# A landing wait in the expert gather: GpSimd issues a pair of rows only when the rows five and six places back have landed

## The reference, cut to what matters

```python
v1, i1 = lax.top_k(s[:, :, 0], PEER_TOPK)      # 16 best of 128 keys, twice
v2, i2 = lax.top_k(s[:, :, 1], PEER_TOPK)
...
sc, p = lax.top_k(cand, PEER_TOPK)             # 16 best of the 256 pairs
eidx = jnp.take_along_axis(cidx, p, axis=-1)
gates = jax.nn.softmax(sc, axis=-1)
ue = u[eidx]
ve = v[eidx]
act = jax.nn.gelu(jnp.einsum('td,thkd->thk', xb, ue).astype(jnp.float32), approximate=False)
return jnp.einsum('thk,thkd->td', (gates * act).astype(x.dtype), ve)
```

## Time and profile before

| | |
|---|---|
| median of 3 runs | 1628.4 us (1625.92 to 1628.66) |
| the profiled execution | 1629.01 us |
| its span, first to last instruction | 1627.2 us |
| mean granted TensorE clock over the span | 0.957 |
| busy: PE, DVE, POOL, ACT | 86%, 63%, 36%, 31% |
| first row of the gather issued, last one issued | 198.59 us, 964.87 us |

### The profile page before, as it was taken

The page is one execution under the profiler, slowest core; times in us unless marked ns, Lnnn a source line. Parts: engine busy times, 40 slices in busy tenths (PEclk is TensorE's granted clock), DMA queues, the critical chain, the costliest instruction groups (busy, mean ns, idle before and its releaser), DMA issues.

```text
span 1627.2 us, 20312 instructions
## 1 busy us (share of the span) xinstructions
PE 1400.7 (86%) x7520; PEld 1041.9 (64%) x7520; DVE 1022.3 (63%) x1818; ACT 497.4 (31%) x846; POOL 586.4 (36%) x630
## 2 busy tenths in 40 slices
PE   8899967977776777587778779999999998999998
PEld 7788956622222222242224329999999997899998
DVE  5995758756546456484744346777877547555444
ACT  2232101211111211121111117554443667544432
POOL 1320055466666666676666550012221002100000
PEclk9999978799998999899999899999999999999999
DMA  9956597799999999999999995758996443245450
GB/s 377 328 209 242 193 370 274 298 366 366 363 370 339 368 365 392 347 368 367 338 371 367 361 352 204 266 207 325 321 317 230 143 150 110 78 156 182 172 188 26
DMA packets 114077, 454.15 MB, mean 279 GB/s; under 512 B 12048, under 2 KB 29600, under 8 KB 100816
## 3 DMA queue, kind: packets, MB, share of 16 engines
q0 software_dynamic: 81616, 297.84, 48.5%
q1 hardware_dynamic: 32384, 155.31, 26.2%
HBM read 452.06 MB, written 1.05 MB: 278 GB/s over the span
## 4 chain that ended last, share of the span: by engine, by line
PE 55%; POOL 12%; issue 11%; DMA 9%; DVE 9%; another core or an unknown queue 3%; ACT 2%; SPq 0%; DVEq 0%; POOLq 0%; ACTq 0%
PE psum L2194 15%; POOL arena L514 12%; PE psum L1818 8%; PE psum L2208 8%; DMA arena<-v_d,arena 7%; PE psum L2089 6%; PE psum L1774 4%; PE psum L1761 3%; DVE arena L1355 3%; PE psum L1849 1%; PE psum L1833 1%; PE psum L1876 1%; PE psum L2049 1%; PE psum L1758 1%
## 5 line engine op out<-in xcount | busy, mean ns | idle before, releaser
L2089 PE MATMUL psum<-arena 128*128 128x512 f32 x952 | 484.4, 643 | 157.4 <-DMA arena<-v_d,arena 109.8
L2089 PEld LDWEIGHTS psum<-arena 128*128 128x128 f32 x952 | 174.7, 199 | 463.8 <-DMA arena<-v_d,arena 261.8
L1355 DVE CUSTOM_DVE_ANT_0 arena<-arena,psum 128x1024 f32<-128x1024 f32 x256 | 304.4, 1219 | 191.1 <-DMA arena<-u_d,arena 158.2
L514 POOL DMA_INDIRECT arena<-u_d,arena x256 | 242.4, 947 | 242.5 <-issue 71.1
L514 POOL DMA_INDIRECT arena<-v_d,arena x256 | 241.1, 942 | 81.9 <-issue 72.9
L741 ACT ACTIVATE arena<-ident,arena 128x128 f32<-128x128 f32 x238 | 84.9, 394 | 445.2 <-PE psum L2089 234.0
L1030 DVE TENSOR_TENSOR wlo<-ring,whi 128x2048 fp32r<-128x2048 f32 x69 | 158.1, 2292 | 86.4 <-ACT whi L582 86.4
L2194 PE MATMUL psum<-xh,whi 128*128 128x256 f32 x704 | 202.1, 287 | 1.3 <-DVE xl L1024 1.0
L2194 PE MATMUL psum<-xl,whi 128*128 128x256 f32 x704 | 199.2, 283 | 0.0
L2194 PE MATMUL psum<-xh,wlo 128*128 128x256 f32 x704 | 199.1, 283 | 0.0
L582 ACT ACTIVATE whi<-ring 128x2048 fp32r<-128x2048 f32 x69 | 131.2, 1902 | 23.7 <-PE psum L1818 18.9
(11 more groups left out here) (309 smaller groups left out, 2317.1 us busy)
## 6 DMA issues: line engine op xcount, KB each, us to landing
ring<-w_ffn SPq DMA_DIRECT2D x44, 1536.0 KB, 6.9
second<-w_ada POOLq DMA_DIRECT2D x64, 384.0 KB, 6.1
arena<-w_ada SPq DMA_DIRECT2D x50, 384.0 KB, 8.5
ring<-w_inproj SPq DMA_DIRECT2D x14, 1024.0 KB, 7.4
ring<-w_qkv SPq DMA_DIRECT2D x12, 1024.0 KB, 4.8
ring<-w_l0in SPq DMA_DIRECT2D x10, 1024.0 KB, 6.8
ring<-w_peerq SPq DMA_DIRECT2D x8, 1024.0 KB, 6.4
sq<-w_ada SPq DMA_DIRECT2D x14, 384.0 KB, 7.4
```

The lines of the kernel that those rows point to most:

```text
L514: g.indirect_dma_start(S["rows"][:, p % GRING, :], None, u_d if kind == "u" else v_d, bass.IndirectOffsetOnAxis(S["idx"][:, n // SLOTS, n ...
L1355: v.tensor_tensor_reduce(row, row, xrow[n // SLOTS], 1.0, 0.0, ALU.mult, ALU.add, S["act"][:, n // SLOTS, n % SLOTS:n % SLOTS + 1]).then_i ...
L2089: ins = t.matmul(vacc[tt][:, at], S["diag"][:, c % DIAGS, :], row[:, at], start=(n % SLOTS == 0), stop=(n == LAST_PE[tt]))
```

## The change

POOL gets one more condition ahead of each pair from p = 6 on: the rows at p - 6 and p - 5 must have landed. It is told by the counts of their semaphores. The circle keeps its 16 buffers, and all other waits stay.

```diff
@@ -61,6 +61,7 @@
 GRING = 16
 DIAGS = 8
+FLIGHT = 6
@@ -511,6 +512,9 @@
                         pool.wait_ge(v_used, pe_count(b))
                     if dve_count(b) > dve_count(a):
                         pool.wait_ge(v_dve, dve_count(b))
+                if p >= FLIGHT and p % 2 == 0:
+                    for q in (p - FLIGHT, p - FLIGHT + 1):
+                        pool.wait_ge(row_in[q % GRING], 16 * (q // GRING + 1))
                 g.indirect_dma_start(S["rows"][:, p % GRING, :], None, u_d if kind == "u" else v_d,
                                      bass.IndirectOffsetOnAxis(S["idx"][:, n // SLOTS, n % SLOTS:n % SLOTS + 1], 0)
                                      ).then_inc(row_in[p % GRING], 16)
```

## The result

The changed kernel took 1619.7 us (median of 12 runs, 1607.6 to 1627.0) and the kernel before 1627.8 us (12 runs, 1620.6 to 1634.1): ratio 0.9947, 95% interval 0.9928 to 0.9966. It is 0.5% faster, 8 us; the forecast was 48 us. The profiled execution took 1615.9 us, with a span of 1614.0.

A forecast was written before the change was run, and what follows sets the result against it. The gather was taken as bound by DMA transfers alternating between full rate and slow stretches after late news; 1629.0 - 41 - 7 = 1581 us, 1580.5 against the median. Forecast range 1555 to 1610 (0.54); 8 in 10: 1545 to 1637.

The forecast's parts named there:

- What bounds the kernel: Gather: bound by row transfers alternating between 1.279 us a row and up to 1.82, as late news stops POOL.
- The cause: Gather: a build-up to over 5 outstanding rows makes news late; the wait cuts 5.2 to 5.6 rows to about 4.5.
- The price of the wait: Paced rows in the gather: 1.35 us each, taken between 1.376 and 1.327, against 1.279 at full rate.
- the rule: POOL's paced pairs: T = (L + 1.98) / 6, T being us a row and L us from issue to landing.
- The main term: Gather from 309.70 to 964.87 us: 455 rows at 1.35 instead of 1.440 us, 41 us less; ends 0 and -73.
- The first part: Gather from 198.6 to 309.7 us, sharing the DMA with weight loads: 7 us less, ends 0 and 27.
- Extra instructions at nothing: POOL: about one added wait instruction per pair costs no time, since the sequencer runs ahead while a row is issued.
- The second: Rival, gather: 4.5 rows still set off the delay, all drains stay, pacing costs extra: 1640 us; slower than 1632: 0.20.
- The third: Rival, main stretch: delays mostly go but the DMA is poorer, T = 1.40 to 1.44: 1610 to 1625 us; chance 0.11.
- The first rival: Gather: something on DVE, not depth, keeps POOL from issuing; the wait only trims draining stretches: 1629 to 1632 us; chance 0.05.
- What would show it: Gather signs: diagonals within 0.1 us, `top_rows` near 3.3 us, short POOL idle, chain rows near 6 us, 380 to 395 GB/s.

The follow-up runs named there:

- first_only_again: The new wait only for rows 6 to 56, against the kernel before, in a session of the quick setting: ratio 1.0001.
- first_only_third: The new wait only for rows 6 to 56, against the kernel before, in a session of the late setting: ratio 0.9928.
- main_only_third: The new wait only from row 57 on, against the kernel before, in a session of the late setting: ratio 1.0014.
- cap8_again: The changed kernel with FLIGHT = 8 instead of 6, against the kernel before, a repeat in the quick setting: ratio 0.9987.
- cap8: The changed kernel with FLIGHT = 8 instead of 6, against the kernel before, first timed in the quick setting: ratio 0.9996.
- cap4: The changed kernel with FLIGHT = 4 instead of 6, against the kernel before, in the quick setting: ratio 1.1858.
- cap5: The changed kernel with FLIGHT = 5 instead of 6, against the kernel before, in the late setting: ratio 1.0365.
- first_only: The new wait only for rows 6 to 56, against the kernel before, first timed in the quick setting: ratio 1.0009.

## Why the prediction was wrong, point by point

**What bounds the kernel: right.** The gather is bound by transfers that alternate, and POOL is stopped by late news. Where the news is never late, rows without a wait run at 1.271 us (first_only_again, which takes as long as the kernel before there), and the kernel before takes 1537 us, 91 us less. So the 1.279 us of the earlier trace rows is about what the DMA gives at best here.

**The cause: half right, and this is the step that failed.** "That the build-up causes the delay is inferred from their coming together", and the sum then let all of it go at 4.5 rows. Two things were wrong in it. The build-up is no sufficient cause: 12 rows outstanding did no harm in the quick setting. And if it is one in the late setting, its onset lies lower than I put it: with the cap at 6 the late waits still stood while 400 GB/s were moved (549 to 572 us), at 5 not. I had put the onset at the smallest depth at which I had seen late news, 5.2 rows, as if the trace had shown that less was safe; the refills it rested on had drained first and showed nothing of a steady 4.5.

**The price of the wait: right in size.** T = 1.35 us a row was forecast for rows paced at 6. Without late news the changed kernel takes 1.352. The wait does bind where nothing is late. That the number came out is in part luck: it was picked between 1.376 and 1.327, of which the second rests on a guessed onset of full rate, and the 1.352 is not the even pace of the rule but a mean over many pairs at 2.4 to 2.7 us and some over 3. FLIGHT = 4 gave 1.865.

**The main term: -41 us forecast, about 0 measured.** It was the difference of 1.440 and 1.35. In the late setting it is 1.433: the paced row's 1.352 and 0.08 us a row, 36 us over 445 rows, of stops that did not go. If the pacing costs in the late setting what it costs in the quick one, the stops shrank from (1.437 - 1.271) x 445 = 74 us to those 36, which saves 38, and the pacing (0.081 x 445) took 36 of it. That split is a calculation across the settings and no run shows it as such. The waits point the same way: POOL's idle before rows that the profile puts down to PE, to DVE's u rows or to "remote", 309.7 to 860 us, is 77.9 us in the kernel before,

```profile
POOL arena L514 <- PE psum L2089: 33.1, 25, 5.3
POOL arena L514 <- DVE arena L1355: 28.7, 13, 5.9
POOL arena L514 <- remote: 16.1, 9, 4.9
```

and 43.0 in the kernel after,

```profile
POOL arena L518 <- PE psum L2093: 24.9, 16, 4.8
POOL arena L518 <- DVE arena L1359: 15.6, 13, 2.5
POOL arena L518 <- remote: 2.5, 1, 2.5
```

while the sum of all its idle has not changed (188 us and 189); in first_only_third and main_only_third the same three are 79.7 and 57.8 us. What is measured without any split is main_only_third, 1.0014.

**The first part: -7 us forecast, 10.5 measured** (first_only_third), inside its ends of 0 and 27. By it and main_only_third the first part carries the whole gain.

**Extra instructions at nothing: right for the time, not for POOL.** In cap8_again, where the wait seldom binds, 99 of 195 pairs from 320 to 860 us start 0.37 to 0.39 us after the issue before, where in first_only_again, which has no wait there, the shortest idle is 0.30 or 0.31. That is 0.04 us a row, and it does not show in the time because POOL still issues a row in about 1.28 us, the DMA's own rate: cap8, which has as many waits, is at 0.9996, 0.9987 and 1.0007 in the quick setting.

**The rivals.** The second was nearest to the late setting: the delay comes under the cap of 6 too. It erred in keeping every stop whole (1640 us); part of them went, about half by the sum above, and that made slower into even. The third named the time (1610 to 1625, T = 1.40 to 1.44) with the wrong reason, a poorer DMA. What I lacked was the case between: the stops shrink and the pacing costs what that saves. The first rival, something on DVE that holds POOL's issues back, fell: issues stayed at a median of 937 ns, and DVE does the same work in the quick setting where nothing is late. The Trainium skill, "SBUF — State Buffer", section "SBUF: two separate sides", has that mechanism; no run here shows a trace of it.

The Trainium skill, "DMA: Bandwidth & Descriptors", section "Anatomy of one DMA — SWDGE (gpsimd) path", gives about 2.0 us plus the bytes at 436 GB/s for one DMA, 3.2 us for one of 524,288 bytes; by my estimate from it three rows outstanding would keep the DMA full. These runs speak against it. A row took longer, as the medians from issue to landing in cap4 show:

```profile
arena<-v_d,arena POOLq DMA_INDIRECT x148, 5.3
arena<-u_d,arena POOLq DMA_INDIRECT x147, 5.0
```

FLIGHT = 6, which lets at most four rows be outstanding when a pair starts and six after it, is at 388 GB/s still short of 409. The 288 GB/s at 4.2 rows that the prediction set against the page were a refill, not a steady depth.

**What would show it.** Listed as right were diagonals within 0.1 us of PE's rows and `top_rows` always near 3.3 us; both are true of the kernel after in the quick setting alone. Chain rows were to be near 6 us: they are (5.87 for the last). The main stretch was to reach 380 to 395 GB/s: 388 in the quick setting, where it is a loss against 409, and 366 in the late one.

**A better version than both:** the wait for rows 6 to 56 only. 0.9928 in the late setting, where the changed kernel has 0.9947 (their intervals overlap), and 1.0009 and 1.0001 in the quick one, where the changed kernel loses 2.2%.

## What stays open

What makes a session late or quick I could not vary; the chip's number does not follow it, and load from outside of the kernel or the place of its tables in memory were not tested. It is no lower ceiling of the DMA: the late setting too has stretches at 410 GB/s. Why the news of PE and DVE is held up while PE goes on with the rows that land, as at 561 to 572 us in the kernel after, no run settled. One other reading can be excluded: that ACT and DVE stand because their own code has yet to be loaded. Such loads are packets of the instruction queues in the DMA view, and in the kernel before, from 424 to 502 us, which holds both long waits of the earlier trace rows, the only queue with packets is that of the rows:

```profile
q0 software_dynamic: 7966, 29.04, 97.2%
```

It is the same from 398.5 to 421.5 us, where ACT's diagonals came late. In the first part too I showed where the gain is, not by which step. The late waits are shorter in the kernel after and in main_only_third than in the kernel before, but no run tells whether by depth or by the pauses that the wait makes.

## What to carry to other kernels

A cap on outstanding transfers is a trade: measure its price where nothing else disturbs, since there it showed as cost alone (here a wait at 8, 6 and 4 rows: 0, 2 and 19%). Two things that come together in one trace are not cause and effect until one of them has been moved alone; and if a cure acts by a threshold, ask whether the trace has ever shown the safe side of it. Put a cap only where it was seen to pay, and time it in more than one session before you keep it.

## What the runs showed of the hardware that I had not expected

- The same program has two settings, 1537 and 1628 us, 6% apart, with the DMA at 409 GB/s in one and 364 in the other. The granted clock over the span is 0.99 in one and 0.96 in the other; the loss itself is in the gather, whose last row landed at 971.85 us in the kernel before and at 879.08 in first_only, while what follows took 655.4 and 653.9 us.
- In the late setting, signals of PE and of DVE to itself came 5 to 10 us late (8.07 for ACT in the earlier trace rows, 5.55 and 9.53 for DVE in the earlier trace rows) while the DMA was near full rate; with 329 GB/s (cap5) DVE had no such wait from 309.7 to 860 us.
- The gather's rate depends on the cap up to eight rows of 512 KB: 282, 388, 407 and 409 GB/s at a wait of 4, 6, 8 and none, all in the quick setting.
